# Start, ScalarE's order in the solve, router and end of a two-layer hybrid decoder trunk

## What is computed

```python
for l in range(2):                       # x: (256 tokens, 1024)
    h = rms_norm(x, norm_mix[l])
    proj = h @ w_in[l]                   # 1024 -> 4120
    y_gdn = gated DeltaNet, 6 heads of 64 (causal conv, l2 norm, chunked triangular solve)
    y_ret = retention, 4 heads (rotary q and k)
    y_mlstm = mLSTM, 6 heads (causal conv, exponential gates)
    x = x + concat(y_gdn, y_ret, y_mlstm) @ w_out[l]
    h = rms_norm(x, norm_ffn[l])
    group = top_1(softmax(h @ router_group[l]))        # 4 groups
    two = top_2((h @ router_expert[l] + router_bias)[group])   # 8 experts each
    x = x + sum over the two: weight * ((silu(h @ gate_e) * (h @ up_e)) @ down_e)   # 32 experts, 256 wide
out = rms_norm(x, norm_final)
```

## Time and profile before

| | before |
|---|---|
| median of 3 runs | 838.24 us (836.58 to 839.73) |
| the profiled execution: its time | 839.36 us |
| its span in the trace | 837.6 us |
| TensorE busy | 783.1 us (94%) |
| VectorE busy | 307.2 us (37%) |
| ScalarE busy | 201.3 us (24%) |
| bytes moved, mean rate | 253.86 MB, 303 GB/s |
| level masks, router weights, parameters | 224, 160 and 154 KB |

### The profile page before, as it was taken

How to read it: one execution, slowest core, us unless ns; L and a number is a source line. 1 busy time by engine, 2 the same in 40 slices (tenths; PEclk the granted TensorE clock), 3 DMA queues, 4 the chain that set the end, 5 groups by cost and what they waited for, 6 DMA issues and landing times.

```text
span 837.6 us, 16668 instructions
## 1 busy us (share of the span) xinstructions
PE 783.1 (94%) x6584; PEld 556.1 (66%) x6584; DVE 307.2 (37%) x733; ACT 201.3 (24%) x427; POOL 4.3 (1%) x13
## 2 busy tenths in 40 slices
PE   4999989999999998799999999899999999999966
PEld 4877778888765554455588778788787555454423
DVE  2757433564421111111177653436624111111102
ACT  2252551442300010001114445326212000001002
POOL 1000000000000000000000000000000000000000
PEclk9999999999999999699999999999999999999998
DMA  9851354486789999999996322645947999999995
GB/s 355 360 176 69 118 188 166 144 325 241 304 360 420 421 420 421 419 423 419 418 418 227 124 103 64 241 156 167 367 191 303 421 420 419 422 421 419 421 421 232
DMA packets 41065, 253.86 MB, mean 303 GB/s; under 512 B 4768, under 2 KB 9376, under 8 KB 11936
## 3 DMA queue, kind: packets, MB, share of 16 engines
q1 hardware_dynamic: 40416, 252.14, 75.4%
q10 hardware_dynamic: 576, 0.72, 0.3%
HBM read 250.35 MB, written 1.44 MB: 301 GB/s over the span
## 4 chain that ended last, share of the span: by engine, by line
PE 70%; DMA 11%; DVE 11%; ACT 3%; issue 3%; DVEq 1%; SPq 0%; ACTq 0%; POOLq 0%
PE ps L1049 13%; PE ps L597 12%; DMA ring<-e_up 10%; PE ps L1019 8%; PE ps L1070 7%; PE ps L921 6%; PE ps L768 4%; PE ps L1078 4%; PE ps L1082 3%; PE ps L813 2%; PE ps L621 2%; DVE xn L1421 2%; DVE work L1540 2%; PE ps L846 1%; PE ps L780 1%
## 5 line engine op out<-in xcount | busy, mean ns | idle before, releaser
L597 PE MATMUL ps<-hT,ring 128*128 128x256 f32 x800 | 183.4, 382 | 0.0
L597 PEld LDWEIGHTS ps<-hT,ring 128*128 128x128 f32 x800 | 148.3, 190 | 22.8 <-issue 3.8
L1019 PEld LDWEIGHTS ps<-work,xn 128*128 128x128 f32 x640 | 77.2, 201 | 10.3 <-issue 8.2
L1019 PE MATMUL ps<-work,xn 128*128 128x128 f32 x640 | 81.0, 288 | 1.9 <-DVE work L1759 1.9
L1049 PE MATMUL ps<-ring,hT 128*32 128x256 f32 x1088 | 67.0, 391 | 7.4 <-DMA ring<-e_up 7.4
L1049 PE MATMUL ps<-work,hT 128*32 128x256 f32 x960 | 59.9, 393 | 8.1 <-DMA work<-e_gate 5.7
L921 PE MATMUL ps<-xn,ring 128*128 128x256 f32 x256 | 57.8, 381 | 0.0
L1049 PEld LDWEIGHTS ps<-ring,hT 128*32 128x32 f32 x1088 | 34.5, 112 | 33.6 <-DMA ring<-e_up 10.5
L921 PEld LDWEIGHTS ps<-xn,ring 128*128 128x128 f32 x256 | 48.1, 190 | 7.2 <-issue 0.7
L1049 PEld LDWEIGHTS ps<-work,hT 128*32 128x32 f32 x960 | 28.9, 112 | 36.2 <-issue 12.1
L1759 DVE TENSOR_TENSOR work<-shapes,sel 128x128 f32<-128x128 f32 x40 | 9.9, 288 | 114.7 <-PE ps L1056 114.4
(11 more groups left out here) (283 smaller groups left out, 843.8 us busy)
## 6 DMA issues: line engine op xcount, KB each, us to landing
ring<-e_up SPq DMA_DIRECT2D x48, 1024.0 KB, 26.2
ring<-w_mix SPq DMA_DIRECT2D x34, 1024.0 KB, 9.6
ring<-e_down SPq DMA_DIRECT2D x32, 1024.0 KB, 26.0
work<-e_gate SPq DMA_DIRECT2D x32, 1024.0 KB, 20.2
more_buf<-e_gate SPq DMA_DIRECT2D x16, 1024.0 KB, 18.6
ring<-e_gate SPq DMA_DIRECT2D x16, 1024.0 KB, 18.7
work<-e_up SPq DMA_DIRECT2D x16, 1024.0 KB, 24.2
shapes<-e_down SPq DMA_DIRECT2D x8, 1024.0 KB, 21.9
```

The costliest lines, as they stand in the source:

```text
L597: mm = pe.matmul(bank, slot_w(i)[:, k, ct * P:(ct + 1) * P], hT3[:, k, :], start=(k == 0), stop=(k == KD - 1))
L1019: mm = pe.matmul(ps[:, 4 + 3 * half_, kk * P:(kk + 1) * P], xn3[:, j, k * P:(k + 1) * P], Psel[:, j, :], start=(j == 0), stop=(j == TT - 1))
```

## The change

The diff has five parts. **Start:** ten matmuls of the ones with themselves (`WARM`) stand ahead of TensorE's first work; slot 0 is loaded in halves, the first between the halves of x; the transfers of level masks and router weights go out behind ScalarE's squares; `first_tile` does tiles 0 and 1 for the first four k, then waits for the whole slot, then tile 0's rest, `ssq`, tile 1's rest. **Solve:** `rotary_in(0)` goes from level 2 to level 3, ahead of the Silu; `rotary_in(1)` and the table load from level 4 to level 5. **Router:** the logits come first, a bank for each token tile; the squares are taken from `xT` by ScalarE, added by VectorE and summed by a matmul (`nsum`); the group's choice uses the unscaled logits; the transposes become products with the identity in banks 0 to 3, which in layer 1 stay there as the accumulators; in layer 0 ScalarE afterwards copies `xT` into the four banks. `start_sums` goes, and the slot in `xT` is released by ScalarE. **Experts:** TensorE waits for `sums_set` ahead of them. **End:** VectorE multiplies the first half of each token tile by the gain ahead of the scale; ScalarE scales the last of them and issues its transfer.

```diff
@@ psum_plan
-    late += [(("xt", 0), 4), (("xt", 2), 6), (("xt", 1), 5), (("xt", 3), 7), ("logits", 0), ("rank", 5)]
+    late += [(("logits", 0), 4), (("logits", 1), 7), ("nsum", 6), ("rank", 5)] + [(("xt", i), i) for i in range(4)]
@@ sync
+            first = loads[0][0][0]
             for j in range(2):
                 sync.dma_start(xT[:, 4 * j:4 * j + 4, :], x_in[:, 4 * j:4 * j + 4, :]).then_inc(x_loaded[j], 16)
+                part = slice(j * SLOT // 2, (j + 1) * SLOT // 2)
+                sync.dma_start(slot[first][:, part], w_mix[0, 0, :, part]).then_inc(arrived[first] if j else first_half, 16)
-                for i in range(NMIX):
+                for i in range(1 - l, NMIX):
...
-            for i, (j, h) in enumerate(((1, 0), (1, 1), (0, 0), (0, 1))):
+            for i, (j, h) in enumerate(((1, 1), (1, 0), (0, 1))):
@@ tensor
-                have_slot(0)
+                if l == 0:
+                    for _ in range(WARM):
+                        pe.matmul(ps[:, 3, 0:P], ones[:, :], ones[:, :], start=True, stop=True)
+                    pe.wait_ge(first_half, 16)
+                else:
+                    have_slot(0)
-                first_tile(0, range(KD))
+                first_tile(0, range(4))
                 first_tile(1, range(4))
+                have_slot(0)
+                first_tile(0, range(4, KD))
...
-                for half_ in range(2):
-                    pe.wait_ge(x_mixed, upto(l, x_mixed, 2 * half_ + 2))
-                    for j in range(TT):
-                        bank = begin(("xt", 2 * j + half_))
-                        for kk in range(4):
-                            mm = pe.transpose(bank[:, kk * P:(kk + 1) * P], xT[:, half_ * 4 + kk, j * P:(j + 1) * P], c("ident"))
-                        done(mm, ("xt", 2 * j + half_))
-                bank = begin("logits")
-                (and its matmuls, start_sums(1), start_sums(0), acc_init and mix_freed)
+                pe.wait_ge(rwg_ready, upto(l, rwg_ready, 1))
+                for j in range(TT):
+                    bank = begin(("logits", j))
+                    for k in range(KD):
+                        if j == 0 and k % 2 == 0:
+                            pe.wait_ge(x_mixed, upto(l, x_mixed, k // 2 + 1))
+                        mm = pe.matmul(bank[:, 0:NLOG], xT[:, k, j * P:(j + 1) * P], rw[:, k, :],
+                                       start=(k == 0), stop=(k == KD - 1))
+                    done(mm, ("logits", j))
+                bank = begin("nsum")
+                pe.wait_ge(x_summed, upto(l, x_summed, 1))
+                for j in range(TT):
+                    mm = pe.matmul(bank[:, j:j + 1], hT3[:, 0, j * P:(j + 1) * P], ones[:, 0:1], start=True, stop=True)
+                done(mm, "nsum")
+                for j in range(TT):
+                    for half_ in range(2):
+                        bank = begin(("xt", 2 * j + half_))
+                        for kk in range(4):
+                            mm = pe.matmul(bank[:, kk * P:(kk + 1) * P], xT[:, half_ * 4 + kk, j * P:(j + 1) * P], c("ident"),
+                                           start=(kk == 0), stop=(kk == 3), skip_group_check=True)
+                        done(mm, ("xt", 2 * j + half_))
...
                 gather(rounds_done(pe, rounds) + l)
+                pe.wait_ge(sums_set, upto(l, sums_set, 4))
@@ scalar
-                    if lev == 2:
+                    if lev == 3:
                         rotary_in(0)
-                    if lev == 3:
                         act.activation(mixT[:, 0:5, :], mixT[:, 0:5, :], ACT.Silu).then_inc(gate_ready, 1)
-                    if lev == 4:
+                    if lev == 5:
                         rotary_in(1)
                         act.preload_act_table_set(LN_EXP)
...
-                    (Square of the transposed banks, with accum_out, for j in range(TT))
+                for n in range(4):
+                    act.wait_ge(x_mixed, upto(l, x_mixed, n + 1))
+                    act.activation(hT3[:, 2 * n:2 * n + 2, :], xT[:, 2 * n:2 * n + 2, :], ACT.Square).then_inc(x_squared, 1)
+                bank = get("nsum")
+                link(act.activation(ss[:, 2:4], bank[:, 0:TT], ACT.Ln, scale=1.0 / D, bias=epsc[:, :]))
...
+                if l + 1 < LAYERS:
+                    for n in range(4):
+                        act.activation(ps[:, n, :], xT[:, 2 * n:2 * n + 2, :], ACT.Copy).then_inc(sums_set, 1)
+                    act.wait_ge(sums_set, upto(l, sums_set, 4))
+                act.sem_inc(mix_freed, 1)
@@ vector
+                for m in (2, 6):
+                    dve.wait_ge(x_squared, upto(l, x_squared, m // 4 * 2 + 2))
+                    link(TTn(hT3[:, m - 2:m, :], hT3[:, m - 2:m, :], hT3[:, m:m + 2, :], ALU.add))
+                link(TTn(hT3[:, 0:2, :], hT3[:, 0:2, :], hT3[:, 4:6, :], ALU.add))
+                TTn(hT3[:, 0, :], hT3[:, 0, :], hT3[:, 1, :], ALU.add).then_inc(x_summed, 1)
                 for j in range(TT):
+                    bank = get(("logits", j))
+                    link(TTn(lg[:, j, 0:8], bank[:, 0:8], pv(l, "router_bias", 0, 8), ALU.add))
                     link(dve.max(rt[:, j, 8:16], lg[:, j, 0:8]))
                     link(dve.max_index(rtx[:, 0, j, :], rt[:, j, 8:16], lg[:, j, 0:8]))
...
+                dve.wait_ge(rstd_ready, upto(l, rstd_ready, 2))
+                (the scaled expert logits, columns 8 on, from both banks)
```

More of the change, by code:

```diff
@@ L46 @@
 RING = 12
+WARM = 10
 SLOT = 2048
@@ L976, in _ @@
                         done(mm, ("xt", 2 * j + half_))
-                bank = begin("logits")
-                pe.wait_ge(rwg_ready, upto(l, rwg_ready, 1))
-                for j in range(TT):
-                    for k in range(KD):
-                        mm = pe.matmul(bank[:, j * HD:j * HD + NLOG], xT[:, k, j * P:(j + 1) * P], rw[:, k, :],
-                                       start=(k == 0), stop=(k == KD - 1))
-                done(mm, "logits")
-                for b in (1, 2, 3):
-                    pe.wait_ge(free[b], upto(l, free[b], uses[b]))
@@ L1333, in _ @@
                 out_rr(7, mrr[:, 2, :])
-                for j in range(TT):
-                    get(("xt", 2 * j))
-                    get(("xt", 2 * j + 1))
-                    b = bank_of[("xt", 2 * j)][0]
-                    link(act.activation(hT[:, j * D:(j + 1) * D], ps[:, b:b + 2, :].rearrange("p b n -> p (b n)"), ACT.Square,
-                                        accum_out=ss[:, j:j + 1]))
-                link(act.activation(ss[:, 2:4], ss[:, 0:2], ACT.Ln, scale=1.0 / D, bias=epsc[:, :]))
+                for n in range(4):
[3 more added lines that the diff above has]
+                link(act.activation(ss[:, 2:4], bank[:, 0:TT], ACT.Ln, scale=1.0 / D, bias=epsc[:, :]))
+                act.sem_inc(free[bank_of["nsum"][0]], 1)
                 act.activation(ss[:, 4:6], ss[:, 2:4], ACT.Exp, scale=-0.5).then_inc(rstd_ready, 1)
@@ L1385, in _ @@
                 act.activation(ss[:, 4 + j:5 + j], ss[:, j:j + 1], ACT.Exp, scale=-0.5).then_inc(final_rstd, 1)
+            act.wait_ge(final_rstd, 2)
+            act.wait_ge(gained_half, 2)
+            act.activation(fin[:, 0, 0:512], fin[:, 0, 0:512], ACT.Copy, scale=ss[:, 4:5]).then_inc(out_first, 1)
+            act.wait_ge(out_first, 1)
+            act.dma_start(out[:, 0, 0:512], fin[:, 0, 0:512]).then_inc(out_done, 16)
         @block.vector
@@ L1710, in _ @@
                     free_(("wo", n))
-                dve.wait_ge(rstd_ready, upto(l, rstd_ready, 2))
-                bank = get("logits")
-                for j in range(TT):
-                    link(dve.scalar_tensor_tensor(out=lg[:, j, :], in0=bank[:, j * HD:j * HD + NLOG], scalar=ss[:, 4 + j:5 + j],
-                                                  in1=pv(l, "router_bias", 0, NLOG), op0=ALU.mult, op1=ALU.add))
-                free_("logits")
+                for m in (2, 6):
[3 more added lines that the diff above has]
+                TTn(hT3[:, 0, :], hT3[:, 0, :], hT3[:, 1, :], ALU.add).then_inc(x_summed, 1)
                 def spread(col, shape):
@@ L1726, in _ @@
                          rtx[:, 0, :, 0:1].to_broadcast([P, TT, 4]), ALU.is_equal))
+                dve.wait_ge(rstd_ready, upto(l, rstd_ready, 2))
+                for j in range(TT):
+                    bank = get(("logits", j))
+                    link(dve.scalar_tensor_tensor(out=lg[:, j, 8:NLOG], in0=bank[:, 8:NLOG], scalar=ss[:, 4 + j:5 + j],
+                                                  in1=pv(l, "router_bias", 8, EXPERTS), op0=ALU.mult, op1=ALU.add))
+                    free_(("logits", j))
                 el = lg[:, :, 8:NLOG].rearrange("p j (g e) -> p j e g", g=GROUPS)
```

52 lines of the change are left out of this document (26 added, 26 removed).

## The result

The changed kernel takes 826.09 us, median of 4 runs (825.84 to 827.74); the kernel before, on the same chip, 837.81 us (4 runs, 836.58 to 839.73). The ratio is 0.9864, with a 95% interval of 0.9845 to 0.9884: faster by 11.7 us. The forecast was 823.4 with a range of 819.5 to 828. So the sign and the range held, and of the forecast gain of 14.9 us some 12 arrived. But the median lies outside the 821.5 to 825 that the prediction gave to its own case A, and nearest to its rivals B (825.7) and C (825.9). The profiled execution is the slowest of the four, 827.74 us with a span of 825.9; before it was 839.36 and 837.6, so the profiles are 11.6 to 11.7 us apart. In all that follows times are from the span's start.

What follows compares the result with a forecast made beforehand. TensorE and its partners bound the mixers, weight transfers the expert stages, whose stream starts with TensorE. Gains of 5.3 + 5.4 + 3.7 + 0.5 = 14.9 us off 839.36 give 824.5, less 1.12 for the median: 823.4, range 819.5 to 828.

Steps and rivals of the forecast that it cites:

- case A: Whole kernel: all four parts gain as forecast, 14.9 us together, giving 821.5 to 825 us; chance 0.60.
- Rival B: Start: the clock has fallen again by the first real matmul, 24 passes take 7.54 us; 825.7 us, chance 0.15.
- Rival C: Sparser TensorE in new router: both layers' first gathers at low clock, 825.9 us; or neither, 821.7; chance 0.15 together.
- Rival F: Expert stream starts by its own clock, only parts behind it count: 0.5 us gained, 837.7 us; chance 0.02.
- DMA idle for under 1 us: Sign ahead of layer 0's experts: the DMA engines would stand idle for less than 1 us.
- Part 1, the start: Kernel start: earlier weights and ten matmuls start the next projection 5.3 us earlier, 3.3 at the slower rate.
- Part 2, ScalarE's order: Solve: moving rotary copies and table load into holes saves 2.7 us a layer, 5.4 in all; bounds 4.0 and 5.8.
- Rival D: Solve: swapped rotary halves land late; with 3 us each, 12 us lost, 835 us; chance 0.06.
- Rival E: Second rotary swap queues behind 1 MB expert loads and eats the 14.9 us; 842.5 us at worst landings; chance 0.02.
- Part 3, the router: Router: group maxima run while the scale is made, gaining 1.85 us a layer, 3.7 in two; bounds 0.5 and 2.2.
- Half of the cover: Router: identity products and ScalarE's copies finish before the gather wants them, with 0.9 us left.
- Part 4, the end: Kernel end: VectorE's last work shrinks by 0.6 us, last transfers share the engines, so 0.5 gained; bounds 0 and 0.9.

Runs made afterwards that it cites:

- the first experiment: Changed kernel again, only a floor of zero put under GpSimd's count of extra rounds: median 826.15 us, ratio 0.9851; the profiled run took 822.62 us.

## Why the prediction was right or wrong

**What bounds the kernel.** Right. The gain of the mixers went into the expert stream as well: the first expert slot is issued 5.7 us earlier, and at the first tile of layer 1 the lead is 6.4. Rival F (only the stream counts) is out, with 12 us gained. One reading was wrong and cost nothing: the 29 us of the earlier trace rows are the transfers' time on the chain and not TensorE's waiting, which for all up projections into the ring was 7.4 us, the longest 2.6. The expert stages kept their length to some tenths of a us: layer 0's is 0.7 shorter, with a gather less slow than before, and in layer 1 the lead is 11.9 when the first experts start and 11.7 at the end. The sign "DMA idle for under 1 us" failed, with some 4 us, and cost nothing that shows.

**Part 1, the start: the mechanism right, the size dependent on the execution.** The first pass at 7.00 against 7.2. The term of 5.3 took the faster rate: 5.8 came in the first experiment's profile (20.22 to 14.42), 4.0 in the one shown, 2.5 without the ten matmuls. Rival B, with 3.3, describes some executions and not the kernel: four of eight profiles with ten matmuls ahead have the slow start. So part 1 was a draw, and the profiled execution drew the slow side. The Trainium skill ("TensorE: Matmul & The Clock Gate", "What's actually happening") says that the number of slow matmuls at a kernel's start varies from run to run; the traces agree, with 5.42 and 7.08 us for the same 24 passes. The forecast read this page for a yes or no, where it should have read it for a chance.

**Part 2, ScalarE's order: right.** 2.82 us in both layers by the traces against 2.7 a layer; alone 6.2 us in the medians against 5.4. The surplus agrees with the clock's fall in level 5 that the old order has in some executions, which the trace of before did not show; that it makes up all of the 0.8 was not shown. Rival D came true in form and not in price, and with it one of the prediction's two signs of being wrong, a new wait for the swaps in VectorE's list: VectorE waits 2.32 us for the second tile, with cover above it. The 0.7 us of slack were reckoned for the first tile, where no wait came. At the second the cover was at least 2.3; over the ten profiles with this order the wait is 0.71 to 2.32 us, and absent once. Rival E would have needed 6.4 us from issue to landing; in layer 0 the longest here was 5.4.

**Part 3, the router: the step that failed.** The prediction says that the identity products take "no more than the 3.68 us of the old ones". They took 6.06 in layer 0 and 3.82 in layer 1, and in 9 of 14 routers of this form 5.45 us or more. The structure's gain was 1.65 to 1.68 us where the clock stood, against 1.85; where it fell the router lost 1.1 against before (identity passes over 6 us) or still gained 0.5 (5.45 us), and in the medians the router alone is worth 0.0, not 3.7. Rival C came nearest in kind (the new router meets a lower clock) and had the wrong place: it looked for the low clock in the first gathers, priced it at 1.6 us and gave both its directions 0.15. The first gathers of the changed kernel are both at full clock; the passes before them are not. That a sparser TensorE is the cause, as C has it, is not shown: in the windows of the fall it is busy throughout. What is shown is that the clock fell in none of four routers with wide passes. Half of the cover held: VectorE, not ScalarE, releases the gather in each trace shown, and ScalarE's four copies into the banks took 0.54 us each and were done by 223.9, not 227.5. But behind the identity passes stand also the passes that take VectorE's mask, which the prediction does not reckon: there only 0.22 us were left, and what the slow passes took beyond that reached the gather.

The Trainium skill ("TensorE: Matmul & The Clock Gate", "PE-mode transpose") holds that a transpose does not count as TensorE being busy in the same way, by which the old router, whose first 16 passes are transposes with 32 passes of 40 columns behind them, should meet the low clock more often than the new one. The traces say otherwise: the old router's products ran at full clock in 8 of 8 cases, and 2 of its 8 gathers were slow (5.45 and 5.39 us). What in the old order of passes keeps the clock was not tried by itself.

**Part 4, the end: the step "both last transfers share the engines, so 0.5" failed.** VectorE's work did shrink, by 0.77 us. But the last bytes are set by four transfers of 1.05 MB together, which take 2.8 us from their first byte on, and the first piece comes no earlier: it waits for the first scale as before. The gain is 0 to 0.2, at the lower bound.

**The sum.** Of the 11.7 us between the two profiles the start has 4.0, the solves 2.8 and 2.8, the routers -1.1 and 1.7, the expert stage of layer 0 0.7, the front of layer 1 -0.6, the first gather of layer 1 1.6, and the rest -0.2. The loss in the front: VectorE's small steps for the gates and the scores come 0.4 and 0.3 us later in the trace of the router alone, and all kernels with the new router have the 0.6. The cause stays open: no kernel tried it by itself. So the forecast was 2.95 us too high in layer 0's router and 1.3 at the start, and 2.3 us came from two places that it did not have. Both are gathers that ran slowly in the profiled execution before: the first of layer 1 (slow in two of the four profiles with the old router) and the one in layer 0's experts (5.81 us against 4.48; over all profiles it is slow in 8 of 14). Without that luck this pair would have shown some 9.4 us. The 823.4 of the forecast is not a state of the kernel with all clocks up; no profile here has that. The profile of 822.62 us, with a fast start and a full clock in layer 0's router but not in layer 1's, stands 14.2 us ahead of before at layer 1's first gather, where the forecast has 14.4, and 16.8 ahead at the end; 1.3 of the 14.2 is layer 0's shorter expert stage, so that even here the sum is right in part by luck.

## What to carry to other kernels

Ahead of trading one TensorE sequence for another, look not only at the number of passes but at the granted clock of the stretch in several executions: here a rewrite that takes 1.7 us off a chain put 1.2 to 2.8 back where that clock fell. Wider passes with unused columns, and some more matmuls ahead of the first, are cheap to try. Then follow the gain to the end of the span: a lead of 1.2 us at layer 1's gather was 0.2 there. Where a kernel's runs fall into two groups, profile one of each before pricing a part: one trace is one draw. And at the end of a kernel ask when the first output piece is ready and how long all bytes take, not when the last one is.

## What the hardware showed that was not expected

- The granted clock fell to 0.50, the 1.2 GHz level, while TensorE was busy in all of each window (1.00 of 1.00 us), in the stretch of 40-column passes (layer 0 of the changed kernel, at 211 to 212), and was back at the full level at 219, in the identity passes that followed.
- In the stretches where transfers set the pace a gather ran slowly in most profiles: in layer 0's experts 4.46 to 5.88 us instead of 3.84 in 8 of 14, the last one 4.36 to 4.91 in 8 of 14, and this in none of the five whose router of layer 1 had been slow.
- 32 passes of 120 columns took 3.80 us, 32 of 40 columns 3.66 at full clock.
- At the start the windows give a granted clock of 1.00 while the same 24 passes take 5.42, 7.08 or 8.18 us, by the profile.
- ScalarE wrote 512 columns from SBUF into a PSUM bank in 0.54 us, and 512 columns from PSUM to SBUF in 0.60 us.
- Four output pieces, 1.05 MB, took 2.8 us from first byte to last, and began 0.8 us after the first was issued.
